# A decoder trunk on 8 cores: the head streams of an HGRN2 mixer issued as two staggered chains instead of pairs in lockstep

## The reference, cut to what matters

```
z = u @ w_in  -> [pool | q | f | i | out_gate | gate_A | gate_B]
q = silu(z_q);  f = lb + (1 - lb) * sigmoid(z_f);  k = 1 - f;  v = z_i
per chunk of 64 tokens (8 for the samples):  b = cumsum(log f)
  qd = q * exp(b);  kd = k * exp(-b);  kt = k * exp(b_last - b)
  o  = tril(qd @ kd^T) @ v + qd @ S;   S = exp(b_last) * S + kt^T @ v
o = o * rsqrt(mean(o^2) + eps) * hgrn_norm_w * silu(z_out_gate)
```

## Time and profile before

| | us |
|---|---|
| median of 3 runs | 2704.28 |
| lowest and highest run | 2652.77, 2735.93 |
| the profiled execution, whole | 2652.0 |
| its span, slowest core (core 1) | 2650.5 |
| spans of the 8 cores | 2613.4 to 2650.5 |
| mean granted TensorE clock | 0.733 to 0.737 of full |
| busy: PE, DVE, ACT, POOL | 1397.1, 1039.1, 708.0, 178.6 |

### The profile page before, as it was taken

How to read it: one execution, slowest core, us unless ns; L and a number is a source line. 1 busy time by engine, 2 the same in 40 slices (tenths; PEclk the granted TensorE clock), 3 DMA queues, 4 the chain that set the end, 5 groups by cost and what they waited for, 6 DMA issues and landing times.

```text
span 2650.5 us, 30702 instructions; the slowest of 8 cores (2613.4 to 2650.5 us)
## 1 busy us (share of the span) xinstructions
PE 1397.1 (53%) x9240; PEld 801.1 (30%) x9240; DVE 1039.1 (39%) x2327; ACT 708.0 (27%) x1276; POOL 178.6 (7%) x165
## 2 busy tenths in 40 slices
PE   1354443377379724444448649763334332581993
PEld 0232222144145412222225326432122221240551
DVE  1344543312422154445442442234555562225225
ACT  3333334333344222333221121012232221112101
POOL 0000100011000000001101000000111110010000
PEclk9676665688689866666669969886566555796996
DMA  7322023556268712000001403313211313331331
GB/s 228 131 96 69 28 80 137 169 178 213 97 201 284 246 45 75 32 33 32 1 32 64 143 17 111 95 33 111 68 60 64 96 33 40 68 124 40 112 104 40
DMA packets 102544, 253.70 MB, mean 96 GB/s; under 512 B 24176, under 2 KB 46960, under 8 KB 92144
## 3 DMA queue, kind: packets, MB, share of 16 engines
q1 hardware_dynamic: 102384, 251.75, 29.8%
HBM read 197.20 MB, written 54.52 MB: 95 GB/s over the span
## 4 chain that ended last, share of the span: by engine, by line
PE 41%; DVE 20%; issue 14%; DMA 13%; ACT 8%; POOL 2%; DVEq 1%; SPq 1%; ACTq 0%; POOLq 0%
PE PS L369 41%; DVE arena L357 11%; ACT arena L364 7%; DVE arena L360 4%; DMA arena<-wada 3%; DMA arena<-xT 2%; DVE arena L354 2%; DMA arena<-win 2%; DMA arena<-wd 2%; POOL arena L357 2%; DMA arena<-wscr 1%; DMA zps<-arena 1%; ACT arena L366 1%; DVEq L150 1%; DVE arena L352 1%
## 5 line engine op out<-in xcount | busy, mean ns | idle before, releaser
L369 PE MATMUL PS<-arena 128*128 128x512 bf16 (+5 forms) x9104 | 1379.4, 311 | 1225.7 <-ACT arena L364 423.8
L369 PEld LDWEIGHTS PS<-arena 128*128 128x128 bf16 x9104 | 789.4, 105 | 1814.1 <-issue 1437.5
L364 ACT ACTIVATE arena<-PS 128x512 f32<-128x512 f32 (+8 forms) x588 | 266.2, 471 | 1151.9 <-PE PS L369 815.8
L364 ACT ACTIVATE arena<-arena 128x128 bf16<-128x128 f32 (+8 forms) x527 | 355.7, 701 | 610.3 <-DVE arena L360 170.6
L357 DVE TENSOR_TENSOR arena<-arena 128x4 f32<-128x4 f32 (+15 forms) x713 | 340.7, 487 | 71.7 <-ACT arena L364 25.3
L357 POOL TENSOR_TENSOR arena<-arena 128x512 bf16<-128x512 f32 (+6 forms) x152 | 175.0, 1154 | 1447.3 <-DVE arena L357 961.0
L357 DVE TENSOR_TENSOR arena<-arena,PS 128x512 bf16<-128x512 f32 (+2 forms) x212 | 117.8, 555 | 311.6 <-PE PS L369 221.0
L360 DVE SCALAR_TENSOR_TENSOR arena<-arena,PS 128x128 f32<-128x128 f32 (+2 forms) x352 | 129.3, 396 | 272.2 <-ACT arena L364 203.9
L375 DVE TENSOR_TENSOR_SCAN arena<-arena 128x512 f32<-128x512 f32 (+2 forms) x48 | 41.2, 901 | 307.3 <-ACT arena L364 307.3
L360 DVE SCALAR_TENSOR_TENSOR arena<-PS,arena 128x512 f32<-128x512 f32 x92 | 57.9, 630 | 193.0 <-PE PS L369 165.1
L366 ACT ACTIVATE arena<-arena 128x512 f32<-128x512 f32 (+4 forms) x136 | 89.8, 696 | 119.6 <-DVE arena L354 118.2
(11 more groups left out here) (9 smaller groups left out, 37.9 us busy)
## 6 DMA issues: line engine op xcount, KB each, us to landing
arena<-wscr SPq DMA_DIRECT2D x112, 512.0 KB, 5.0
wscr<-arena SPq DMA_DIRECT2D x56, 512.0 KB, 9.1
arena<-win SPq DMA_DIRECT2D x26, 1024.0 KB, 7.9
arena<-wada SPq DMA_DIRECT2D x24, 1024.0 KB, 6.7
arena<-xT SPq DMA_DIRECT2D x32, 384.0 KB, 5.8
arena<-wg SPq DMA_DIRECT2D x11, 1024.0 KB, 8.5
arena<-wu SPq DMA_DIRECT2D x11, 1024.0 KB, 8.5
arena<-wd SPq DMA_DIRECT2D x16, 704.0 KB, 6.7
```

Of the source, the lines that this page charges most:

```text
L364: K.op("act", lambda e: e.activation(out=out, in_=in_, func=func, scale=scale), r, w)
L369: K.op("pe", lambda e: e.matmul(out, lhsT=lhsT, rhs=rhs, start=start, stop=stop), r, w)
```

## The change

The two heads of a pair no longer start each tile together. Two chains are made: one runs heads 0, 2, 4, 6 with the buffers `HS[0]`, the other heads 1, 3, 5, 7 with `HS[1]`, each head with all its tiles, without a meeting point between tiles or pairs. The first chain emits 16 steps before `zip_run` alternates the two. In pass 2 each chain runs the sample tile of a head itself, behind the head's prompt tile and in the buffers of its own set (but for `D1`, where the narrow set's is used since its zero columns lie elsewhere), and a flag keeps the two chains' sample tiles apart. The two units of a head are fetched when its chain comes to it, not four at the start of a pair.

```diff
+STAGGER = 16
...
-                ACT(cs_(B.D1[:, :n]), cs_(B.rP[:, :n]), AF.Identity, r=[B.trP], w=[B.tD1])
+                D1b, tD1b = (SS.D1, SS.tD1) if is_s else (B.D1, B.tD1)
+                ACT(cs_(D1b[:, :n]), cs_(B.rP[:, :n]), AF.Identity, r=[B.trP], w=[tD1b])
...
-                SCAN(B.P[:, :n], B.rP[:, :n], B.D1[:, :n], r=[B.trP, B.tD1], w=[B.tP])
+                SCAN(B.P[:, :n], B.rP[:, :n], D1b[:, :n], r=[B.trP, tD1b], w=[B.tP])
...
-            for hp in range(4):
-                h0, h1 = 2 * hp, 2 * hp + 1
-                get_units(h0)
-                get_units(h1)
-                for ti_, (c0_, n_, _) in enumerate(ptgs):
-                    gl = [head_stream(h0, HS[0], c0_, n_, False), head_stream(h1, HS[1], c0_, n_, False)]
-                    if last and ti_ == len(ptgs) - 1:
-                        gl.append(chain(head_stream(h0, SS, plen, 128, True), head_stream(h1, SS, plen, 128, True)))
-                    zip_run(gl)
+            sbusy = [False]
+
+            def stream_chain(heads, B):
+                for h_ in heads:
+                    get_units(h_)
+                    for (c0_, n_, _) in ptgs:
+                        yield from head_stream(h_, B, c0_, n_, False)
+                    if last:
+                        while sbusy[0]:
+                            yield
+                        sbusy[0] = True
+                        yield from head_stream(h_, B, plen, 128, True)
+                        sbusy[0] = False
+
+            gA = stream_chain([0, 2, 4, 6], HS[0])
+            gB = stream_chain([1, 3, 5, 7], HS[1])
+            for _ in range(STAGGER):
+                next(gA)
+            zip_run([gA, gB])
```

## The result

The changed kernel takes 2558.46 us (median of 10 runs, 2552.37 to 2682.07), the kernel before 2678.74 (10 runs, 2648.91 to 2749.15). The ratio is 0.9657, 95% interval 0.962 to 0.9694: **3.4% faster**. The runs of both lie in two groups some per cent apart, and comparisons use the lower group alone. The profiled execution's span is 2554.9 us against 2650.5: 95.6 us less. The prediction had 2593 from its sum, 59 less than the 2652.0 of before, and wrote 2600.

A forecast was written before the change was run, and what follows sets the result against it. It took the head stages as bound by a chain of waits passing between engines. Gains of -30, -24 and -5 us in passes 0, 1 and 2 sum to -59: 2593 from 2652.0, written as 2600, range 2535 to 2690.

The forecast's parts named there:

- Projections of the first chain's 512 tile: Passes 0 and 1: projections with the other's attention and transposes between, eviction and column split, 11.0 us of the period.
- Scan, reciprocal, KD and QD with two updates between: First chain's 512 tile, passes 0 and 1: these with two of the other's state updates between, 7.2 us.
- State steps: Passes 0 and 1: eight at 1.1 us, update 0.3 plus three of the other's tiny dependent instructions 0.8, total 8.9.
- Newton to cast: First chain's 512 tile: Newton held for the other's scan, then behind its reciprocal, 11.3 us, 3.5 its own work.
- Some twenty hand-offs between engines: Passes 0 and 1: hand-offs at 0.1 us each, added as 2 us to the 79 of a period.
- the four waits: Lockstep head stages before the change: idle waits of DVE and PE, put at 36 of the 88.7 us period.
- the overlap works better: Rival, passes 0 and 1: clock holds through alternating groups, Newton not held for the scan; period 75, 2545 us, chance 0.13.
- The lead-in: Start of head stages: first scan at 80.0 us in pass 0, and 9 us earlier in pass 1.
- Pass 2: Third head stage: two blocks of 48 us make a pair of 96 against 95.8; only the ends gain, -5 us.
- The slow clock: Rival: PE's split projection groups never reach clock 1.00, 13.6 us more a period, 94.6; 2732 us, chance 0.1.
- late sample state: Rival, pass 2: with one `S0` buffer the load lands 10 us late in six blocks; 2653 us, chance 0.03.
- the queues holding each other more than seen: Rival: each of 48 steps waits 0.1 us more for the other chain; period 86, 2635 us, chance 0.27.

The follow-up runs named there:

- STAGGER 0: The changed kernel with the first chain's head start set from 16 steps to 0; ratio 0.9952 against the kernel before, lowest 2636.57 us.
- unbroken Newton run: The changed kernel with the three Newton rounds, cast and diagonal matrix emitted in one step, three empty steps behind; lowest 2571.66 us.
- STAGGER 8, 12 and 24: The changed kernel with the first chain's head start set from 16 steps to 8, 12 or 24; ratios 0.9831, 0.9875 and 0.984 against the kernel before.

## Why the prediction was right, and where it was off

**Direction, place and mechanism** were right: all gain in the head stages, from the bursts and the DVE chains falling apart; projections of one stream beside the tail of the other; Newton rounds with a scan and a reciprocal inside; nothing outside. STAGGER 0 shows that the offset is the cause. DVE's longest wait in passes 0 and 1 is 5.8 us, under the 6 forecast.

**The size** was too small: -59 forecast, 0.6 of the -96 measured. 2558.46 is inside the whole range, but under the 2565 to 2620 of the forecast itself and nearer to the rival's 2545. The terms that were mis-sized are those of the period, 81 against 75.0. In the rows of pass 1 the first chain's 512 tile takes 44.3 (1030.6 to 1074.9) and not 48.2, the 256 tile 28.7 (1077.5 to 1106.2) and not 28.3, and 2.1 lie between tiles, not 2.5 + 2:

- Projections of the first chain's 512 tile, with 1.7 for a slow start: the granted clock was 1.00 there, and start of burst (1030.6) to scan took 9.2, not 11.0. For the second chain, whose burst starts at 0.50, the 11.0 fits: 10.8, from 1054.9 to 1065.7.
- Scan, reciprocal, KD and QD with two updates between: 6.1 (1039.8 to 1045.9), not 7.2.
- State steps: 1.1 in the 512 tile against 0.97, and 4.9 for four in the 256 tile against 3.3 (first at 1091.45, last to 1094.72). I had added the partner's three small instructions in full; without them updates of one chain stand 0.59 to 0.72 us apart (1076.81, 1077.40; 1038.20, 1038.92), so they cost 0.25 to 0.4 and not 0.8.
- Newton to cast: 11.3 against 9.6. That it was held was right (3 us by waiting for and doing the scan, 3.3 by the reciprocal).
- "Some twenty hand-offs between engines": 2 us that the durations taken from the rows held already.

Against these, Newton and broadcast of the 256 tile were set 2.4 us too low, and the diagonal matrix and broadcast of the 512 tile took 4.0 and not 2.5. So errors of both signs stand in the 81, and part of them cancels. One sum was wrong and carried nothing: the four waits of 15.81, 7.42, 11.36 and 7.83 make 42.4 of the 88.7 us, not 36. The rival "the overlap works better" had the period, 75, and 2545. Of its two reasons one was right in small part (the clock held at one of four bursts) and one wrong: Newton was still held for the scan. The unbroken Newton run shows that freeing it would not have brought what the rival counted on.

**The lead-in** was right: first scan of pass 0 at 80.16 us, 80.0 forecast; pass 1's came 19.0 after its fence, 8 earlier than before, where 9 was forecast.

**Pass 2**: 96 a pair forecast, 92.05 measured, and that near only because errors cancel. Of a block's 48 the state steps with the sample's chain had 15.5 and took 13.6 and 13.0 (1834.7 to 1848.3, 1881.3 to 1894.3), and the 2 of hand-offs did not come. But the sum left out the output matmuls up to the sums (2.7 and 2.6), and the diagonal matrices up to the gate product took 3.9, not 2.0. In the state steps I chose 4.56 for VEXP because it runs with POOL; the trace has it at 2.28:

```profile
1836.14 2.28 DVE L358 TENSOR_TENSOR arena<-arena 128x2048 bf16<-128x2048 bf16 x1
...
1842.09 0.69 DVE L358 TENSOR_TENSOR arena<-arena,PS 128x512 f32<-128x512 f32 x1 [3.41 <-POOL arena L358]
```

It does run with POOL. POOL's scaling of `S0`, timeline of POOL, before and then after:

```profile
2054.34 3.64 POOL L357 TENSOR_TENSOR arena<-arena 128x2048 f32<-128x2048 f32 x1 [6.36 <-ACT arena L364]
```

```profile
1837.44 4.47 POOL L358 TENSOR_TENSOR arena<-arena 128x2048 f32<-128x2048 f32 x1 [4.09 <-ACT arena L365]
```

Before, POOL was first: VEXP (2055.57) began with 2.41 us of POOL's 3.64 left and took 2.28 longer. After, VEXP is first (1836.14), and POOL, which began with 0.98 of it left, takes 0.83 longer. The two took turns in both cases, 5.8 us from the start of the first to the end of the second, and the adds come behind the second. So the rows show 4.56 with no wait of the adds for POOL, or 2.28 with a wait of 3.41; my 15.5 took the 4.56 and named the wait for POOL beside it. All eight of the pass, groups by line, engine and form (busy us and mean ns behind the first bar) in the windows of the stage, before and after:

```profile
L357 DVE TENSOR_TENSOR arena<-arena 128x2048 bf16<-128x2048 bf16 x8 | 27.4, 3420 | 0.0
```

```profile
L358 DVE TENSOR_TENSOR arena<-arena 128x2048 bf16<-128x2048 bf16 x8 | 18.3, 2284 | 0.0
```

A mean of 3420 ns is four at 4.56 and four at 2.28; after, all eight are at 2.28. That is 9.1 of the 12.9 us that DVE is busy less. The adds still wait 3.41 for POOL.

**The slow clock** (0.1) and the late sample state (0.03) did not come; the queues holding each other more than seen (0.27) neither, at this offset. STAGGER 8, 12 and 24 have periods of 82 to 85, near that rival's 86, and my walk didn't say how narrow the place at 16 is. Why 12 is 10 us a period worse than 16 is shown only in part (3.4 in the state updates of one tile).

## What to carry to other kernels

Two streams zipped step by step gain from an offset, but in-order queues make the gain depend on which instructions meet. The one difference that was traced (12 against 16) says that a chain of short, latency-bound steps should stand beside the partner's short steps and not beside its long matmul groups. Count the offset from the partner's nearest tile too, but no rule of distance told the best one, so measure several: here 0, 8, 12, 16, 17, 19 and 24 give periods of 88.5, 84.8, 85.4, 75.0, 78.1, 76.8 and 82.2 us. Look in every stage for a lockstep that the new order makes again; the one between prompt and sample was worth more (45 us of stage 2) than the change had won there (10).

## What was not expected of the hardware

DVE and POOL can hold each other for a whole instruction, and the one that starts second pays. A DVE tensor_tensor or scan from SBUF that starts while POOL's tensor_tensor runs was longer by what was left of POOL's, less about 0.14 us: VEXP by 2.28 with 2.41 left (before), the scan of the unbroken Newton run by 0.83 with 0.98 left (2.06 and not 1.23), and in the first sample after the change a 128x4 product at 1797.67 took 3.60 us and not 0.16, with 3.58 left. POOL paid in the same way when it came second: 4.47 and 5.59 for the scaling of `S0`, 3.64 alone. The bank product, which has an input in PSUM, was not held (0.69 at 1074.17 with 0.69 of POOL's left), nor was the reciprocal of 128x128 (0.94 at 1878.22 with 1.00 left). So a price for such an instruction has to say which of the two starts first.

The reciprocal of 128x512 takes 3.35 us, 2.7 times the scan of the same tile, and half of it left out was worth 51 us of the kernel.
